# Gates and branch projections of two mixers: weights stationary or tokens stationary, in a two-block transformer kernel on one Trainium2 core

## The reference, cut to what matters

```
u = norm(h);  z = u @ w_in          # 3072 of its columns are the gates
gates = sigmoid(z_gate).reshape(b, s, 3, 1024)
merged = sum over n of gates[n] * (branch[n] @ w_branch[n])     # 512 -> 1024 each
h = h + merged @ w_out                                          # 1024 -> 1024
```

## Time and profile before

| | |
|---|---|
| median of 3 runs | 2118.26 us (2118.0 to 2118.33) |
| the profiled execution, its own time | 2119.66 us |
| its span, first to last instruction | 2117.9 us |
| mean granted clock of PE | 0.997 of full speed |
| PE busy | 2094.0 us (99%), 14136 matmuls |
| DVE busy | 1261.6 us (60%) |
| ACT busy | 1038.0 us (49%) |
| bytes read from HBM | 372.49 MB, 176 GB/s over the span |

### The profile page before, as it was taken

One profiled execution on the slowest core, in us unless ns is written; L12 is line 12 of the kernel. 1 busy time (PEld: TensorE's weight loads), 2 busy tenths in 40 slices (PEclk: granted clock), 3 DMA queues, 4 the chain that ended last, 5 costly groups with the idle time before them and its releaser, 6 DMA issues.

```text
span 2117.9 us, 32417 instructions
## 1 busy us (share of the span) xinstructions
PE 2094.0 (99%) x14136; PEld 1931.1 (91%) x14136; DVE 1261.6 (60%) x1399; ACT 1038.0 (49%) x1327; POOL 91.0 (4%) x123
## 2 busy tenths in 40 slices
PE   8999999999999999999999999999999999999998
PEld 7998989989989898899898989999899889998897
DVE  5555576665555555766654565556755656567555
ACT  5444476454444345665443356643544466444442
POOL 1000100000000001000000000010100000100000
PEclk9999999999999999999999999999999999999999
DMA  8555444465555555444565564544655545455552
GB/s 295 189 190 181 161 144 140 140 209 188 190 193 201 196 172 186 147 140 140 180 206 197 161 225 140 175 140 155 239 187 191 197 145 177 146 174 199 183 196 80
DMA packets 178206, 375.65 MB, mean 177 GB/s; under 512 B 8480, under 2 KB 18848, under 8 KB 178064
## 3 DMA queue, kind: packets, MB, share of 16 engines
q1 hardware_dynamic: 174256, 360.67, 51.4%
q0 software_dynamic: 3808, 12.90, 1.9%
HBM read 372.49 MB, written 1.05 MB: 176 GB/s over the span
## 4 chain that ended last, share of the span: by engine, by line
PE 96%; DMA 1%; DVE 1%; ACT 0%; issue 0%; SPq 0%; POOL 0%; POOLq 0%; DVEq 0%
PE pb L1438 51%; PE pb L1421 37%; PE pb L1448 1%; DMA raw<-in_ffn_w_up_dram 1%; PE pb L1493 1%; PE pb L1546 0%; PE pb L1501 0%; PE pb L1502 0%; PE pb L1500 0%; DVE wl L1837 0%; DMA raw<-in_w_in_dram 0%; PE pb L1545 0%; ACT wh L1642 0%; PE pb L1609 0%; PE pb L1568 0%
## 5 line engine op out<-in xcount | busy, mean ns | idle before, releaser
L1837 DVE TENSOR_TENSOR wl<-raw,wh 128x2048 fp32r<-128x2048 f32 (+3 forms) x348 | 781.0, 2250 | 288.4 <-ACT wh L1642 288.0
L1642 ACT ACTIVATE wh<-raw 128x2048 fp32r<-128x2048 f32 (+3 forms) x348 | 654.7, 1882 | 478.0 <-PE pb L1421 225.1
L1438 PE MATMUL pb<-xh,wl 128*128 128x256 f32 x2752 | 789.0, 287 | 0.0
L1438 PE MATMUL pb<-xl,wh 128*128 128x256 f32 x2752 | 779.6, 283 | 0.0
L1438 PE MATMUL pb<-xh,wh 128*128 128x256 f32 x2752 | 779.5, 283 | 0.0
L1438 PEld LDWEIGHTS pb<-xh,wl 128*128 128x128 f32 x2752 | 528.7, 192 | 4.2 <-issue 3.0
L1438 PEld LDWEIGHTS pb<-xh,wh 128*128 128x128 f32 x2752 | 528.8, 192 | 1.0
L1438 PEld LDWEIGHTS pb<-xl,wh 128*128 128x128 f32 x2752 | 528.6, 192 | 0.0
L1421 PE MATMUL pb<-wl,mh 128*128 128x512 f32 x736 | 253.8, 391 | 0.3
L1421 PE MATMUL pb<-wh,mh 128*128 128x512 f32 x736 | 252.7, 389 | 0.0
L1421 PE MATMUL pb<-wh,ml 128*128 128x512 f32 x736 | 252.7, 389 | 0.0
(11 more groups left out here) (344 smaller groups left out, 1813.9 us busy)
## 6 DMA issues: line engine op xcount, KB each, us to landing
raw<-in_w_in_dram SPq DMA_DIRECT2D x100, 1024.0 KB, 5.2
raw<-in_w_ff_dram SPq DMA_DIRECT2D x64, 1024.0 KB, 5.1
raw<-in_ffn_w_up_dram SPq DMA_DIRECT2D x44, 1024.0 KB, 5.1
raw<-in_ffn_w_down_dram SPq DMA_DIRECT2D x44, 1024.0 KB, 5.0
raw<-in_ffn_w_gate_dram SPq DMA_DIRECT2D x42, 1024.0 KB, 5.1
raw<-in_w_branch_dram SPq DMA_DIRECT2D x24, 1024.0 KB, 5.0
raw<-in_w_out_dram SPq DMA_DIRECT2D x16, 1024.0 KB, 5.0
raw<-in_w_in_dram SPq DMA_DIRECT2D x4, 832.0 KB, 4.4
```

What stands on the lines that cost most here:

```text
L1438: ins = e.matmul(o, w[:, n, c], x[:, it["kk"] + n, :], skip_group_check=True, start=(it["first"] and n == 0 and q == 0 and f % 2 == 0), st ...
L1642: e.activation(hi, raw, ACT.Copy).then_inc(m.high_done, 1)
L1837: e.tensor_tensor(lo, raw, hi.bitcast(F32), ALU.subtract).then_inc(m.low_done, 1)
```

## The change

The gates and the branch projections go from the features form to the tokens form, with the same units in the same order. `G` and `mT` then hold tokens on the partitions, at column `t * 1024 + 512 * j`, and the ACT and DVE instructions on them keep their shape of 128 x 512. Each branch is one group of two units; the last branch of a mixer has `end=True`, so that it visits (unit 0, t 0), (unit 1, t 0), (unit 0, t 1), (unit 1, t 1). As the way out needs the merged tile with features on the partitions, each quarter of it (`t`, `j`) is turned after its last merge: a generator in lane 1 + t waits one tick and then turns four tiles into slots 4j to 4j + 3 of `mh` and `ml`. The splits of `mT` by `split_into` go away.

```diff
@@ Memory.tile
+        if name == "mT":
+            return self.mT[:, t * D + (4 * src[2] + c) * P:t * D + (4 * src[2] + c + 1) * P]
@@ Memory.pair_of
-        if name == "mT":
-            return self.mT[:, i * S:(i + 2) * S]
@@ Plan
     def gates(self, name, l, c0, slot):
         for j in range(2):
-            def epi(i, p, use, j=j):
-                self.add("gate", i=i, j=j, p=p, use=use, slot=slot, free=self.g_free[slot])
-                self.g_use[slot, i, j] = use
-            self.turned_group("X", [(name, (l,), 512 * i, 4, c0 + 512 * j, 512) for i in range(2)], self.pair(j), epi)
+            def epi(t, p, uses, j=j):
+                self.add("gate", t=t, j=j, p=p, use=uses[0], slot=slot, free=self.g_free[slot])
+                self.g_use[slot, t, j] = uses[0]
+            self.group(self.cols(name, l, c0 + 512 * j, j, epi))
 
     def branch(self, name, l, n, Y, base, slot, first, last):
         def epi(j):
-            def f(i, p, use):
+            def f(t, p, uses):
+                use = uses[0]
                 done = ("evac", use) if first else ("gated", self.next("gated") + 1)
-                self.add("merge", i=i, j=j, p=p, use=use, slot=slot, gate=self.g_use[slot, i, j], first=first,
-                         before=self.m_done.get((i, j)))
-                self.m_done[i, j] = done
+                self.add("merge", t=t, j=j, p=p, use=use, slot=slot, gate=self.g_use[slot, t, j], first=first,
+                         before=self.m_done.get((t, j)))
+                self.m_done[t, j] = done
                 self.g_free[slot] = done
                 if last:
-                    self.split_into(4 * j + 2 * i, ("mT", 4 * j + 2 * i), done)
+                    self.lanes[1 + t].append(turn(t, j, done))
             return f
-        for j in range(2):
-            self.turned_group(Y, [(name, (l, n), 0, 4, 512 * j, 512)], self.pair(j), epi(j), base)
+
+        def turn(t, j, done):
+            yield
+            self.turn("M", 4 * j, t, ("mT", t, j), 4, [done], max(self.m_free[4 * j + c] for c in range(4)))
+        self.group([dict(key=(name, (l, n), 0, 4, 512 * j, 512), X=Y, slots=list(range(base, base + 4)),
+                         segs=[(j, 0, 512)], first=True, last=True, epi=epi(j)) for j in range(2)], end=last)
@@ act_program, gate
-            f = 4 * it["j"] + 2 * i
+            o = t * D + 512 * it["j"]
...
-            e.activation(m.GT[it["slot"]][:, f * S:(f + 2) * S], bank[:, :], ACT.Tanh,
+            e.activation(m.GT[it["slot"]][:, o:o + 512], bank[:, :], ACT.Tanh,
@@ dve_program, merge
-            f = 4 * it["j"] + 2 * i
-            G, mT = m.GT[it["slot"]][:, f * S:(f + 2) * S], m.mT[:, f * S:(f + 2) * S]
+            o = t * D + 512 * it["j"]
+            G, mT = m.GT[it["slot"]][:, o:o + 512], m.mT[:, o:o + 512]
```

## The result

The changed kernel takes 2110.14 us in the median of 6 runs (2108.82 to 2113.8), the kernel before 2118.13 us (6 runs, 2117.46 to 2119.17). The ratio is 0.9964, with a 95% interval of 0.9954 to 0.9974: 8.0 us, or 0.4%, faster. The forecast was 2108.5 us, 0.5% faster, in a range of 2103.5 to 2113.5. Another five runs of it, beside a later set, gave a median of 2110.44 us against 2118.12, ratio 0.9963 (0.9951 to 0.9976).

What follows compares the result with a forecast made beforehand. The prediction took PE's issue of matmuls to bound the kernel. Its terms, -21.8 + 3.4 + 7.4 + 1.2 = -9.8 us, took the median from 2118.3 to 2108.5 us, range 2103.5 to 2113.5.

Steps and rivals of the forecast that it cites:

- What bounds the kernel: PE, busy for 2094.0 of 2117.9 us: the kernel ends when PE has issued all of its matmuls.
- Part 1: Gates and branches: 3456 matmuls become 1728 of twice the columns, each with about 13 ns fixed: 21.8 us less.
- Part 2: Gates and branches: 76 interruptions of PE's main stream by lanes, each 0.045 us dearer: 3.4 us more (2.3 to 4.6).
- Part 3: Merged tile: 16 added turns of four transposes, 0.46 us each: 7.4 us more, without waits.
- Part 4: Tanh, merges, splits of the turned bank, fetches and queues: no cost, and five `wh` buffers still suffice.
- Part 5: Small work of ACT and DVE beside visits shortened to 2.72 us: PE waits 1.2 us more, bounds 0 and 3.
- The sum: Whole kernel: -21.8 + 3.4 + 7.4 + 1.2 = -9.8 us, so the profiled execution's 2119.66 us becomes 2109.9.
- From the sum to the median: Whole kernel: profiled execution is 1.4 us above the median; the median should become 2118.3 - 9.8 = 2108.5 us.
- The range: Whole kernel: 2104 us with cheap interruptions and no lost cover, 2113 with upper bounds for interruptions, turns and lost cover.
- A: First stack's gates and branches: heads' chains, not PE, set the pace, giving back 2 x 5.45 us: 2118.2; chance 0.08.
- B: Gates and branches: tokens matmuls at 0.233 us, 2118.9, or the skill's fixed part, 2126.0; chance for both 0.04.
- C: Turns and way out: waits for merging behind weight splits, 7.2 us per mixer, 29 in all: 2137; chance 0.04.

Runs made afterwards that it cites:

- experiment 1: The changed kernel with each matmul of the gates and branches cut into two of 256 columns: 2125.84 us, ratio to the kernel before 1.0031.
- e2_no_turn: The changed kernel without the 16 turns of the merged tile, its quarters split untransposed by the old split, which fills slots for both token halves: 2115.05 us.
- e6_alternate: The changed kernel with the last branch alternating between the two token halves (no `end=True`): 2110.22 us, ratio to the kernel before 0.9964.
- e5_eager_turn: The changed kernel with each turn directly behind the visit that fills its bank, no tick between: 2143.36 us, ratio to the kernel before 1.0115.
- experiment 8: The changed kernel run and profiled once more with no edit, giving its second profile: 2110.44 us.
- experiment 4: The same run as e5_eager_turn, the changed kernel with no tick ahead of each turn: 2143.36 us.

## Why the prediction was right, point by point

- **What bounds the kernel:** right. No DMA or split became late, DVE and ACT were nowhere the bound, and the stages changed by PE's sequence.
- **Part 1, 21.8 us less:** right in its cause (experiment 1) and size. The rate after is 0.2272 us, as taken. The Trainium skill's 2.5 ns ("TensorE: Matmul & The Clock Gate", section "Back-to-back issue gap") would have made the kernel slower; no run here agrees with it (0.1199 and 0.1200 us at 256 columns, 0.2272 at 512). The section gives that figure for a matmul by itself, without a budget for weight loads.
- **Part 2, 3.4 us more:** right in kind, some 0.9 too high. I compared each interruption of the gates-and-branches stages before and after, from the last main start ahead of it to the last start before the next one. The 12 of a second-stack stage are 0.030 us dearer in the mean, the 20 or so of a first-stack stage that hold no wait 0.044 us, close to my 0.045. The scores of rows 7, at 306 us, went from 0.64 to 309.60 - 306.20 - 12 x 0.227 = 0.67 us:

```profile
306.20 0.39 PE L1426 MATMUL pb<-wh,xl 128*128 128x512 f32 x1
...
309.60 0.39 PE L1426 MATMUL pb<-wh,xl 128*128 128x512 f32 x1
```

The entry into a second-stack stage is 0.12 us cheaper, which I had not thought of. Together 2.5 us.
- **Part 3, 7.4 us more:** 7.4 by the stages, 7.8 to 8.1 by the medians; no wait, with 1.1 us to spare as worked out.
- **Part 4, nothing:** right, DVE and ACT busy times are within 1 us of before. The five `wh` buffers sufficed: PE's list has no wait for `wh` or `wl`. What I had not seen is that the order `end=True`, which holds unit 0 for three visits, fits the way out only because the turned tile becomes ready by token half (e2_no_turn); it gains nothing over alternating (e6_alternate).
- **Part 5, 1.2 us more:** right in the first profile, too low in the second. The lost cover stands in two kinds of place. At the lone heads' transposes, four times, the interruption is 0.36 to 0.40 us dearer, as PE waits 0.3 us in each: 1.5 us. I had put four such places at 0.1 us each, and they are others than the one I read. At the first head pair of a mixer it depends on the half-clock stretch ahead: -0.2 us per mixer in the first profile, where in the second layer's mixer the stretch that went gave back 1.54 us and the waits that came took 1.38; 0.2 and 0.4 us more in the second. Together 1.1 us in the first profile and 2.1 in the second.
- **The sum:** for the changed part of the kernel, -21.8 + 2.5 + 7.4 + 1.1 and 0.2 less elsewhere give the -11.0 us of the first profile, and with 2.1 in place of 1.1 the -10.0 of the second, against the forecast -9.8. So the mechanism came out term by term; that the second comes as near as 0.2 is luck in part, as Part 2 was 0.9 too high and Part 5 0.9 too low. The executions themselves differ by 10.1 us (2119.66 to 2109.59) and 9.2 (2110.44), as both profiles of the changed kernel start their first mixer 0.8 to 1.0 us later.
- **From the sum to the median:** this step was off. By medians the change is 7.7 to 8.0 us. I took the profiled execution of the kernel before, which is 1.5 us above the median beside the changed kernel, and supposed that the changed kernel's would lie as far above its own; it lies 0.6 below. The granted clocks of the other executions say why in part. They are 0.998 in the median of 36 executions of the kernel before and 0.997 in that of 11 of the changed one; the profiles with one stretch in the mixers and with two have these two values, so by this estimate the median execution has about one stretch before and two after. At like clock the mean spans are 8.9 us apart at 0.999 (2116.0 and 2107.1), 8.1 at 0.997 (2117.1 and 2109.0). Eleven executions are few, why the changed kernel falls to half clock more often stays open, and so does 1 us or so.
- **The range:** 2104 and 2113 are not what my bounds add up to. Parts 2, 3 and 5 at their lower ends give 2106.2, at their upper ends 2115.5 (2118.3 - 21.8 + 4.6 + 11.4 + 3). The result lies inside either.
- **The rivals:** A is what happened in small, 1 to 2 us of its 10.9; B did not happen; C did not, and e5_eager_turn shows that its waits were one tick away.

## What to carry to other kernels

Where PE issues without a gap, count matmuls as well as columns: with a stationary tile of its own, each costs about 13 ns here beyond its columns (at 256 and at 512), and the same product in half as many matmuls of twice the columns is 5% cheaper. Take this for results that are used as they lie; where the result must be transposed, the turns may eat it all, as they did for the branches. And when the main stream gets faster, the small work that was hidden behind a fixed number of its steps loses cover: look for its smallest slack first, and don't expect to mend it by moving one step, since the lanes share the same engines.

## What was not expected of the hardware

A wait and a half-clock stretch can stand for each other. After the 2.1 us that PE waits for `kT`, some executions go on at clock 0.50 for 3.4 us and others don't, in the same kernel; where PE slows, the next wait disappears (18 places, experiment 8). Such a stretch costs 1.55 us where nothing waits behind it (experiment 4), but 0.5 us here. Single spans of this kernel are worth no more than 1 to 2 us.

Plain float32 transposes are interruptions of the main stream beyond their own length: four take 0.44 us up to the second matmul behind them before either form, and another 0.02 us spreads over the following matmuls of the tokens form, as intervals of up to 0.236 us instead of 0.227, where the features form takes 0.01 back in intervals of 0.116 to 0.119 instead of 0.120 (at 640 and 652 us of the kernel before).
